# A hybrid decoder step: the state scan's steps stand between pieces of the projection, the expert gathers follow the first block alone, and the rest runs among them

## The reference, cut to what matters

```python
q, k, v, u = split(x @ w_in + b_in)                  # 1024 -> 4 x 512
att  = merged dilated causal windows over q, k, v     # 8 heads; decode reads cache_k, cache_v
ssm  = Re(C h) + D u,  h = complex diagonal scan of u # 32 groups, 64 states each
z = gelu(ssm); ssm_out = z * sigmoid(z @ w_glu + b_glu)
h = LN1(ALPHA * x + concat(rms(att), rms(ssm_out)) @ w_out + b_out)
# PEER: for each token 8 heads x 16 experts of 16384
q2 = h @ w_pq; s1, s2 = q2 against sub_keys1, sub_keys2
e, g = top 16 of the sums of the two top 16s          # 128 experts per token
ffn = sum(g * gelu(h . peer_u[e]) * peer_v[e])
y = LN2(ALPHA * h + ffn + sigmoid(h @ w_ple_gate) * (p @ w_ple))
```

## Time and profile before

| what | us |
|---|---|
| median of 3 runs | 2127.41 (2124.93 to 2131.17) |
| the profiled execution: its own time | 2128.64 |
| its span, first to last instruction | 2126.5 |
| first gather issued | 553.3 |
| last gather issued | 2097.2 |
| busy: PE | 1553.9 (73%) |
| busy: DVE | 1326.6 (62%) |
| busy: POOL, ACT | 795.9 (37%), 690.3 (32%) |
| bytes moved | 693.19 MB, of which gathers 604.02 MB |

### The profile page before, as it was taken

How to read it: one execution, slowest core, us unless ns; L and a number is a source line. 1 busy time by engine, 2 the same in 40 slices (tenths; PEclk the granted TensorE clock), 3 DMA queues, 4 the chain that set the end, 5 groups by cost and what they waited for, 6 DMA issues and landing times.

```text
span 2126.5 us, 23002 instructions
## 1 busy us (share of the span) xinstructions
PE 1553.9 (73%) x7124; PEld 789.1 (37%) x7124; DVE 1326.6 (62%) x3148; ACT 690.3 (32%) x2472; POOL 795.9 (37%) x816
## 2 busy tenths in 40 slices
PE   8988989999976676777666686566577656667654
PEld 6566765465443343334333433122222222122111
DVE  3328871227778888878888877754544455444554
ACT  0012232221334444444444443233333333223332
POOL 0013336200244444444444444454343444444442
PEclk9998999999888787888878887678888788778887
DMA  7010017882499999989999989999997999989996
GB/s 301 1 53 1 1 58 318 337 306 112 174 388 418 396 412 403 400 348 403 414 409 406 411 343 418 406 399 391 411 394 315 393 410 406 419 364 378 423 422 278
DMA packets 99094, 693.19 MB, mean 326 GB/s; under 512 B 10800, under 2 KB 15664, under 8 KB 21936
## 3 DMA queue, kind: packets, MB, share of 16 engines
q0 software_dynamic: 82944, 604.02, 69.9%
q1 hardware_dynamic: 16048, 87.89, 10.6%
HBM read 687.00 MB, written 4.87 MB: 325 GB/s over the span
## 4 chain that ended last, share of the span: by engine, by line
PE 41%; DMA 25%; DVE 18%; issue 8%; ACT 4%; POOL 3%; POOLq 0%; ACTq 0%; DVEq 0%; SPq 0%
DMA R<-d_uv,E 24%; PE bank L921 13%; DVE R L1667 6%; PE bank L599 4%; PE bank L712 4%; PE bank L871 3%; PE bank L815 3%; POOL R L560 3%; PE bank L852 3%; PE bank L898 2%; PE bank L593 2%; PE bank L648 1%; PE bank L664 1%; ACT E L1220 1%; DVE E L1603 1%
## 5 line engine op out<-in xcount | busy, mean ns | idle before, releaser
L921 PE MATMUL bank<-R,E 128*32 128x512 f32 x2304 | 736.1, 812 | 507.2 <-ACT E L1225 498.9
L560 POOL DMA_INDIRECT R<-d_uv,E x576 | 686.6, 1192 | 1027.0 <-PE bank L921 556.2
L1667 DVE CUSTOM_DVE_ANT_0 R<-R,E 128x1024 f32<-128x1024 f32 x576 | 692.0, 1223 | 430.2 <-DMA R<-d_uv,E 414.5
L921 PEld LDWEIGHTS bank<-R,E 128*32 128x32 f32 x2304 | 237.4, 134 | 954.8 <-ACT E L1225 688.5
L1217 ACT ACTIVATE E<-E 128x2 f32<-128x2 f32 x288 | 57.8, 201 | 350.4 <-DVE E L1667 346.3
L1225 ACT ACTIVATE E<-E 128x32 f32<-128x32 f32 x576 | 153.6, 313 | 9.4
L871 PEld LDWEIGHTS bank<-E,W 128*128 128x128 f32 x1280 | 144.4, 192 | 19.1 <-issue 17.7
L871 PE MATMUL bank<-E,W 128*128 128x128 f32 (+1 forms) x1280 | 148.0, 276 | 1.1 <-ACT E L1128 1.1
L1220 ACT ACTIVATE E<-E 128x1 f32<-128x1 f32 x576 | 138.2, 287 | 12.4
L1168 ACT CAST E<-E 128x4 uint32<-128x4 f32 (+1 forms) x146 | 27.8, 191 | 340.5 <-DVE E L1667 340.4
L599 PE MATMUL bank<-E,W 128*128 128x288 f32 x384 | 95.3, 412 | 8.9 <-DMA E<-d_xT 8.9
(11 more groups left out here) (280 smaller groups left out, 1733.2 us busy)
## 6 DMA issues: line engine op xcount, KB each, us to landing
R<-d_kc SPq DMA_DIRECT2D x8, 2560.0 KB, 12.4
R<-d_vc SPq DMA_DIRECT2D x8, 2560.0 KB, 10.0
R<-d_uv,E POOLq DMA_INDIRECT x576
W<-d_w_pq SPq DMA_DIRECT2D x4, 2048.0 KB, 16.8
W<-d_w_in SPq DMA_DIRECT2D x3, 2048.0 KB, 15.8
R<-d_w_out SPq DMA_DIRECT2D x2, 2048.0 KB, 8.3
W<-d_w_gate SPq DMA_DIRECT2D x2, 2048.0 KB
E<-d_xT SPq DMA_DIRECT2D x2, 1152.0 KB, 8.5
```

Of the source, the lines that this page charges most:

```text
L560: pool.indirect_dma_start(ring[r], None, A["uv"], bass.IndirectOffsetOnAxis(ap=stage[:, half, s:s + 1], axis=0),).then_inc(landed[r], 16)
L921: last = mm(acc[p0:p0 + TG, half * 512:half * 512 + 512], wsel[:, r, :], ring[r][:, D + half * 512:D + half * 512 + 512], start=False, sto ...
L1667: last = nc.vector.tensor_tensor_reduce(ring[r][:, 0:D], ring[r][:, 0:D], hrep[:, js[s], :], 1.0, 0.0, ALU.mult, ALU.add, dots[:, x, s:s + 1])
```

## The change

The diff is 2,297 lines long; what follows says what moves, and the diff under it is cut to the parts that decide it.

**Ahead of the gathers** one list, `FRONT`, takes the place of the hand-written loops. The projection is cut into pieces: u, q and k into 8 pieces each (one tile of 128 channels for 288 tokens), v into 5 (one block each, its bias now added by a one-row matmul). The 8 pieces of u come first, then the 16 steps of the scan, with two pieces between a step and the next in steps 0 to 7 and one piece of v in steps 7 to 11. Attention of block 0 alone (8 units) stands in steps 8 to 12. The four products with the rotation tables are all on DVE. The B matrices of the scan are no longer padded with zeros: a matmul of `ssm_in` uses 32 rows. All copies out of the projection are on ACT. The decode tokens' state recurrence on POOL stands among the carries. After step 12 the gated unit, after step 13 `project_first` for block 0, and after the last step the residual, the norm, the gated unit of blocks 1 to 3, all four `ask`s of block 0, and its first pick. POOL's loop has no wait on `out_full` any more: the first gather follows the first pick (`first_stage`).

**Among the gathers**, at half turns given by a table: attention of blocks 1 to 3 (24 units, two to a half turn, half turns 0 to 16), picks 1 to 3 every 6 half turns, projection and norm of blocks 1 to 3 (17 to 24), picks 4 to 15 every 4 (24 to 72), decode (from 64, a sequence every 3), the decode tokens' gated unit, projection and norm (91 to 101), the last block's picks (105 to 121), and the gates and `finish` of the five blocks (from 118, one every 4). Since the buffers of the cache, of `w_out` and of `w_pq` are now shared with other data, `w_out` is loaded three times and `w_pq` in part three times.

```diff
+PIECES = [(kind, c, x) for kind in "uqk" for x in range(2) for c in range(CT)] + [("v", b, 0) for b in range(BLOCKS)]
+LAST_WIDE = 6 * CT
+ATT_STEP = 8
+UNITS = [(qb, h) for qb in range(QB) for h in range(NH)]
+
+
+def order_of_front():
+
+
+    steps = 4 * QB
+    pieces = {n: [2 * CT + 2 * n, 2 * CT + 2 * n + 1] for n in range(2 * CT)}
+    pieces[ATT_STEP - 1].append(LAST_WIDE)
+    pieces.update({ATT_STEP - 1 + b: [LAST_WIDE + b] for b in range(1, BLOCKS)})
+    order = [("piece", n) for n in range(2 * CT)] + [("tm", 0), ("tm", 1)]
+    order += [("ssm_in", 0, s) for s in range(4)] + [("s_in",)]
+    for n in range(steps + 1):
+        k = n - ATT_STEP
+        now = [2 * k, 2 * k + 1] if 0 <= k < NH // 2 else []
+        was = [2 * k - 2, 2 * k - 1] if 1 <= k <= NH // 2 else []
+        p = pieces.get(n, [])
+        following = [("ssm_in", n + 1, s) for s in range(4)] if n + 1 < steps else []
+        order += [("scores", i) for i in now] + [("bias", i) for i in now] + [("exps", i) for i in now]
+        order += [("values", i) for i in was] + [("piece", x) for x in p[0:1]] + following[0:1]
+        order += [("norm_out", i) for i in was]
+        if n < steps:
+            order.append(("scan", n))
+        order += [("turn_probs", i) for i in now[0:1]] + following[1:2]
+        order += [("invert", i) for i in now] + [("copy_pt", i) for i in now[0:1]]
+        order += [("piece", x) for x in p[1:]] + following[2:3]
+        if n >= 1:
+            order.append(("ssm_out", n - 1))
+        order += [("turn_probs", i) for i in now[1:2]] + [("copy_pt", i) for i in now[1:2]] + following[3:4]
+        if n >= 1:
+            order.append(("skip_term", n - 1))
+        if n + 2 < steps:
+            order.append(("tm", n + 2))
+        if n == 5:
+            order.append(("gelu", 0))
+        if n == 10:
+            order += [("s_ssm_out",), ("s_skip_term",)]
+        if n == 12:
+            order += [("squares", 0), ("turn_att", 0), ("att_out", 0), ("glu_first",), ("gate_first",),
+                      ("product_first",)]
+        if n == 13:
+            order += [("keep_squares", 0), ("sums_first",), ("rms", 0), ("rms_root", 0), ("project_first",),
+                      ("rms_inverse", 0)]
+    order += [("gelu", 1), ("residual", 0), ("root", 0), ("normal", 0), ("glu_rest",), ("gate_rest",),
+              ("turn", 0), ("ask", 0, 0), ("ask_out", 0, 0), ("match", 0, 0), ("match_out", 0, 0),
+              ("ask", 0, 1), ("ask_out", 0, 1), ("match", 0, 1), ("match_out", 0, 1), ("free", 2),
+              ("spread", 0, 0), ("spread", 0, 1)]
+    for c in (2, 3):
+        order += [("ask", 0, c), ("ask_out", 0, c), ("match", 0, c), ("match_out", 0, c), ("free", 2)]
+    order += [("tops", 0, 0, 0), ("tops", 0, 0, 1), ("cross", 0, 0), ("resolve", 0, 0), ("lay", 0, 0), ("first_stage",),
+              ("alpha",)]
+    return order
...
+DECODE_AT = 64
+DECODE_TURNS = 3
+SAMPLE_AT = DECODE_AT + DECODE_TURNS * (NB - 1) + 7
+TURN_AT = SAMPLE_AT + 10
+PICK_AT = TURN_AT + 3
+GATE_AT = PICK_AT + 13
+GATE_TURNS = 4
+FINISHED = [2, 0, 1, 3, 4]
...
+    at[0] += [("product_rest",), ("sums_rest",), ("free", 2)]
+    at[1].append(("take_sums",))
+    for k in range((QB - 1) * NH // 2):
+        two = [NH + 2 * k, NH + 2 * k + 1]
+        qb = two[0] // NH
+        at[k] += [("scores", i) for i in two]
+        at[k + 1] += [("bias", i) for i in two] + [("exps", i) for i in two] + [("turn_probs", i) for i in two]
+        at[k + 2] += [("invert", i) for i in two] + [("copy_pt", i) for i in two] + [("values", i) for i in two]
+        at[k + 3] += [("norm_out", i) for i in two]
+        if two[1] % NH == NH - 1:
+            at[k + 3] += [("squares", qb), ("turn_att", qb)]
+            at[k + 4].append(("att_out", qb))
+            at[k + 5].append(("keep_squares", qb))
...
+    for n in range(1, 4):
+        pick(n, 6 * (n - 1))
+        at[6 * (n - 1) + 5].append(("lay", *picks[n]))
+
+    t = NORM_AT - 1
+    at[t] += [("rms", 1), ("rms_root", 1)]
+    for b in range(1, QB):
+        u = t + 2 * (b - 1)
+        if b == 1:
+            at[u + 1].append(("rms_inverse", 1))
+        at[u].append(("project", b, 0))
+        at[u + 1] += [("residual_half", b, 0), ("project", b, 1)]
+        at[u + 2] += [("residual_half", b, 1), ("root", b)]
+        at[u + 3].append(("normal", b))
+    at[LOOK_AT - 3].append(("turn", 1))
...
+    for b in range(NB):
+        t = DECODE_AT + DECODE_TURNS * b
+        for k, what in ((0, "s_scores"), (1, "s_scores_rest"), (2, "s_bias"), (3, "s_exp"), (4, "s_norm"),
+                        (5, "s_turn"), (6, "s_copy"), (7, "s_values"), (8, "s_copy_out"), (9, "s_turn_out"),
+                        (10, "s_out")):
+            at[t + k].append((what, b))
...
+    for k, b in enumerate(FINISHED):
+        t = GATE_AT + GATE_TURNS * k
+        at[t].append(("gate_turn", b))
+        at[t + 1].append(("gate", b, 0))
+        at[t + 2] += [("gate_out", b, 0), ("gate", b, 1)]
+        at[t + 3].append(("gate_out", b, 1))
+        if b < QB:
+            at[t + 5].append(("finish", b))
...
+            sp.wait_ge(y_full, 4 * QB)
+            for c in (1, 2, 3):
+                load(parts_of[0][c], eight(A["w_pq"][c]), in_pq[c])
+            sp.wait_ge(out_full, 1)
+            load(parts_of[0][0], eight(A["w_pq"][0]), in_pq[0])
...
+            sp.wait_ge(pq_full, 4 * QB)
+            keys(0)
+            load(sbias[0:ST], A["sbias"], in_sb)
+            values(0)
+            for b in range(1, NB):
+                keys(b)
+                if b >= 2:
+                    values(b - 1)
+            sp.wait_ge(ss_full, NB)
+            load(s_wout[0], eight(A["w_out"][0]), in_out[0])
+            load(s_glu_w, A["glu"], in_glu)
...
-                        last = mm(bank[:, 6 + x, j * P:j * P + P], Bt[:, 4 * q + j, x, :],
-                                  uT[:, q, b * P:b * P + P], start=True, stop=True)
-                last.then_inc(bu_full, 1)
+                    j = (step + x) % 4
+                    r = slice(32 * j, 32 * j + 32)
+                    last = mm(bank[:, 6 + x, j * P:j * P + P], Bt[r, q, x, :], uT[r, q, b * P:b * P + P],
...
-                tt(turned[n % 2][1], t2, s_, ALU.mult)
-                tt(turned[n % 2][3], t2, c_, ALU.mult).then_inc(im_turned, 1)
...
-                tt(p_rc, t1, c_, ALU.mult)
+                tt(p_rc, t2, c_, ALU.mult)
                 after(m_im)
-                tt(p_rs, t1, s_, ALU.mult).then_inc(hs_ready, 1)
+                stt(p_rs, t2, -1.0, s_, ALU.mult, ALU.mult).then_inc(hs_ready, 1)
+                tt(p_is, t4, s_, ALU.mult)
+                tt(p_ic, t4, c_, ALU.mult).then_inc(im_turned, 1)
...
-            pool.wait_ge(out_full, BLOCKS)
```

More of the change, by code:

```diff
@@ L172, in order_of_work @@
-    experts(1)
-    order.append(("lay", *picks[-1]))
-    def gate(b):
-        experts(1)
-        order.append(("gate_turn", b))
-        experts(2)
-        for half in range(2):
-            order.append(("gate", b, half))
-            experts(1)
-            order.append(("gate_out", b, half))
-            experts(2 if b < 2 else 3)
-    for b in range(3):
-        gate(b)
-        order.append(("finish", b))
-    gate(3)
-    gate(4)
-    experts(4 * block + 2 - turn)
-    order.append(("finish", 3))
```

1434 lines of the change are left out of this document (803 added, 631 removed).

## The result

| | us |
|---|---|
| before, median of 6 runs | 2131.36 (2124.93 to 2134.27) |
| changed, median of 6 runs | 2113.55 (2105.63 to 2114.83) |
| ratio changed to before | 0.9915, 95% interval 0.9896 to 0.9934 |
| changed, profiled execution: own time, span | 2109.89, 2108.1 |
| first gather, last gather issued | 338.0, 2079.6 |

A forecast was written before the change was run, and what follows sets the result against it. Bound by PE's chain of waits before the first gather, by DMA after it. First gather 355, stretch 1741 and 16.5 behind the last landing make a 2112.5 span, adjusted to 2113 us; range 2060 to 2175.

The forecast's parts named there:

- First gather: Front, summed along PE's order: first gather goes out at 355 us, 198 earlier; bounds 340 and 390.
- Stretch: First gather to last landing: grows from 1556.7 to 1741 us by moved loads and engine work.
- Bytes: Among the gathers: 71.5 MB of cache, weights and other rows move there, 172 us at 415 GB/s.
- the sign that I had named for a sum that is too small: Among the gathers: a rate under 400 GB/s beside loads would mean bytes cost more than the 172 us.
- Attention and projection: Half turns 0 to 16 and 17 to 22: engine work adds 15 us and 5 us.
- Gates: End of the gathers, every four half turns: PE work with `finish` adds 8 us in all.
- Decode: A sequence every three half turns: 0 us beyond its counted bytes, bounds 0 and 15.
- The 8 us of idle time to be filled: Among the gathers: moved loads fill a sixth of the 47 us of idle DMA time, 8 us off.
- the first rival: Half turns 0 to 16: ACT and DVE work holds up the ring, +42 us with gates' share, 2155; chance 0.23.
- A late first gather: Front, steps 8 to 16: waits between engines put the first gather at 395, total 2153; chance 0.10.
- Loads filled idle time: Among the gathers: moved bytes take the idle 47 us, attention costs nothing, 40 us less, 2073; chance 0.16.
- The switch of table: Attention's 13 half turns: ACT table switches cost twice their 1.28 us load, 33 us on top, 2146; chance 0.04.

The follow-up runs named there:

- the second profile: The changed kernel itself, nothing altered, measured and profiled again on another chip: 2104.84 us, ratio 0.9919 to the kernel before.
- the run with more of ACT: Changed kernel plus three more 128x256 exponentials on ACT for each of 24 attention units among the gathers: 2100.62 us, ratio 0.9901.
- the fastest version: Changed kernel with first-asked w_pq part loaded first, first pick ahead of asks 2 and 3, each sequence's keys loaded in two parts: 2050.00 us, ratio 0.9638.

## Why the prediction was right, and where it was not

The time came out at 2113.55 against 2113, and the mechanism is the one forecast: a front shortened by some 200 us, paid back by bytes. But the front was 17 us shorter and the stretch 13 longer than forecast, and that the total comes out within 1 us is luck.

- **First gather: 338 against 355.** The eight pieces of u end at 41.7 (41). The next steps are where it failed: step 7 ends at 145 and not at 163. I took `ssm_out` at 2.5 from the earlier trace rows and 0.4 for switching; its loops stand in another order in the changed kernel, which I had not looked at, and it takes 1.08, and PE switches without a gap. Period 11.0, not 12.9. Steps 8 to 11 took 56 (60), steps 12 to 16 took 54 (53), the loads of `w_pq` 23 (22.5), and from the first ask to the first gather 59 (56). This last part has the wait of 21.7 us of DVE for ACT, which I had not seen: I wrote that the pick needs only the first two asks and lies beside the others, where ACT's order puts its exponential behind them. It did not spoil the sum only because I let all four asks stand in PE's row. The 54 of steps 12 to 16 is right as a sum but not by its working: the scans of steps 11 to 15 start at 188.6, 199.3, 215.6, 226.4 and 244.8, not 8.5 apart with DVE leading. DVE waits 5.4 us for ACT ahead of the third of them, and 9.4 for an `ssm_out` that stands on PE behind `project_first` ahead of the last.
- **Stretch: 1754 against 1741**, and 1743 in the second profile. Bytes: 72.5 MB more by rate and time, where I had 71.5: right. The mean rate is 391 to 394, as I had, but the sign that I had named for a sum that is too small, a rate under 400 beside the loads, came too: 387 and 394 in half turns 64 to 95. Attention and projection, 20 us by my sum: half turns 0 to 23 took 36 and 31 more than before, of which the 13.6 MB loaded there are 33 at 411 GB/s. So they cost next to nothing, and the run with more of ACT shows that the cover is real. Gates: 8 by my sum, 17 and 14 in the table. Decode: 0 by my sum, bounds 0 and 15, beside its bytes; its 41 MB are 100 us at 411 GB/s, and it took 114 and 103 more. Half turns 24 to 63 were not in my sum and took 6 and 12 more at the same bytes, with the share down from 0.99 to 0.97; why, no run shows. The 8 us of idle time to be filled were filled in one place: half turns 96 to 117 moved 15 MB more (37 us at 411 GB/s) in 25 us more (27 in the second profile), their share going from 0.95 to 0.99. Decode and the gates lost more than that by waiting, and the mean share stayed at 0.97.
- **The rivals.** The ring did get held up by the engines, as the first rival has it, but in decode and in the gates and not in half turns 0 to 16 where I put it, and beyond my terms for 11 to 23 us (14 and 5 in decode, 9 and 6 in the gates), not 42. A late first gather did not come. Loads filled idle time in half turns 96 to 117 alone, 10 to 12 us of the 40 of that rival. The switch of table shown above costs 1.3 us, not 2.7.
- What the change could have had: the two waits in the front and the loop of the key buffer lay in the order of the jobs and in the order of SP's queue. Measured each on one chip, they are 26 and 9 us; the 0.9638 of the fastest version against 0.9915 would be 59, but across chips.

## What to carry to other kernels

When a kernel becomes bound by DMA in one stretch, loads that stand in a stretch with idle DMA engines are free, and moving them is not: price each byte that a change moves across that border before you count what the earlier start brings. In a list of jobs that each engine goes through in order, look for the job that waits for late data ahead of the one that frees buffers (here scores ahead of the expert sums on PE, and copies of later asks ahead of the first pick's exponential on ACT). When a load beside a full queue is late, count its packets as well as its bytes. Two errors can make a right total: compare the terms. And compare versions on one chip: the same kernel on two may differ by more than the edit is worth.

## What the runs showed of the hardware

- Sixteen matmuls, each with a weight matrix of 128 rows and 32 columns (32 records in all), took 1.08 us when four successive ones wrote to four different groups of 32 partitions of the bank, and 2.46 when four successive ones added up in the same group, at the same granted clock (1.00) and operands.
- A load issued beside the gathers took 27 to 30 us for 2560 KB of keys with 2560 KB of values ahead of it (768 packets), 20 to 22 us without the values (512 packets), and 31 to 34 us for an eighth of the bytes of both (1792 packets). Beside the 768, 512 and 1792 packets the gathers moved 795 to 855, 670 to 789 and 1398 to 1505 packets of 8 KB.
- A switch of ACT's table took 1.28 us with the next activation 0.02 us behind and the copy ahead ended 0.01 us before.
- The same kernel differed by 1% between measurements on two chips (0.9782 and 0.9686 of the kernel before); in the profiled executions the difference stood in the stretch with two limits. The kernel before differed by 0.1% between the same two (2124.34 and 2125.72).
